# Sums of squares folded on GpSimd, a half tile for the last index columns, and one step moved a slot later in a three-block transformer kernel

## The reference, cut to what matters

```python
def rms_norm(x, g):
    xf = x.astype(jnp.float32)
    y = xf * lax.rsqrt(jnp.mean(xf * xf, axis=-1, keepdims=True) + EPS)
    return (y * g.astype(jnp.float32)).astype(x.dtype)

# block 1: norms, a linear recurrence over chunks (RWKV) and a banded attention
#          beside each other, gates, two branch products, an output product
# block 2:
h = rms_norm(x, norm1_g[l])
proj = jnp.einsum('btd,dc->btc', h, w_in[l])   # q k v | qi (8 heads of 64) ki (64) wi (8) | u v | gates
s = jnp.einsum('bqhd,bsd->bqhs', qi, ki)        # index scores, then top_k picks the keys
score = jnp.einsum('bqh,bqhs->bqs', wi * idx_scale, jax.nn.relu(s))
# ... sparse attention over the picked keys, spatial gating, gates ...
x = x + merged @ w_out[l]
h2 = rms_norm(x, norm2_g[l])
x = x + jnp.square(jax.nn.relu(h2 @ w_ff1[l])) @ w_ff2[l]
x = rms_norm(x, final_g)
# block 3: rmsnorm, input product, pooled mixer and dilated attention, a norm on each,
x = x + jnp.concatenate([y_pool, y_attn], axis=-1) @ w_out[l]
x = x + jnp.square(jax.nn.relu(rmsnorm(x, norm_mlp_g[l]) @ w_up[l])) @ w_down[l]
return rmsnorm(x, norm_final_g)
```

## Time and profile before

| | us |
|---|---|
| median of 3 runs | 3521.14 (3518.85 to 3521.15) |
| the profiled execution | 3520.25 |
| its span, first to last instruction | 3518.5 |
| PE busy in the span | 3405.9 (97%) |
| DVE busy | 2206.8 (63%) |
| ACT busy | 1553.8 (44%) |
| POOL busy | 283.8 (8%) |
| mean granted TensorE clock | 0.986 of full |

### The profile page before, as it was taken

The page is one execution under the profiler, slowest core; times in us unless marked ns, Lnnn a source line. Parts: engine busy times, 40 slices in busy tenths (PEclk is TensorE's granted clock), DMA queues, the critical chain, the costliest instruction groups (busy, mean ns, idle before and its releaser), DMA issues.

```text
span 3518.5 us, 52977 instructions
## 1 busy us (share of the span) xinstructions
PE 3405.9 (97%) x22306; PEld 2958.6 (84%) x22306; DVE 2206.8 (63%) x3056; ACT 1553.8 (44%) x2142; POOL 283.8 (8%) x313
## 2 busy tenths in 40 slices
PE   8999999998989999999999999999999899999998
PEld 7888878777878888788888888888888788888887
DVE  5567655556667576777676446655777766456644
ACT  4445333334543445444544334444444444334444
POOL 3100122220011101101100000001000000000000
PEclk9999999999989999999999999999999999999999
DMA  6554333335634555555555655555554455555654
GB/s 191 183 170 155 129 116 113 109 106 180 193 119 156 186 158 171 168 156 179 185 182 187 195 188 189 191 192 188 164 164 156 156 191 192 191 179 186 198 186 137
DMA packets 587492, 592.47 MB, mean 168 GB/s; under 512 B 20901, under 2 KB 581365, under 8 KB 587126
## 3 DMA queue, kind: packets, MB, share of 16 engines
q1 hardware_dynamic: 587254, 589.08, 52.2%
HBM read 582.72 MB, written 6.32 MB: 167 GB/s over the span
## 4 chain that ended last, share of the span: by engine, by line
PE 89%; DVE 6%; ACT 2%; issue 1%; DMA 1%; SPq 0%; POOL 0%; ACTq 0%; DVEq 0%; POOLq 0%
PE gp L2385 53%; PE gp L2391 28%; PE sidep L1068 4%; DVE w_parts L2314 2%; ACT w_parts L2307 1%; PE sidep L526 0%; DMA high<-bias_rows 0%; DVE stage L2027 0%; ACT lo_half L1940 0%; DVE stage L2031 0%; PE sidep L1308 0%; DMA ring<-w_branch_rwkv 0%; PE sidep L1386 0%; SPq L2141 0%; PE sidep L1645 0%
## 5 line engine op out<-in xcount | busy, mean ns | idle before, releaser
L2314 DVE TENSOR_TENSOR w_parts<-ring,w_parts 128x1024 fp32r<-128x1024 f32 x1084 | 1365.2, 1282 | 427.5 <-ACT w_parts L2307 426.0
L2385 PE MATMUL gp<-x_parts,w_parts 128*128 128x512 f32 x5856 | 1520.8, 400 | 18.5 <-issue 10.6
L2307 ACT ACTIVATE w_parts<-ring 128x1024 fp32r<-128x1024 f32 x1084 | 1108.5, 1053 | 411.6 <-PE gp L2391 405.4
L2385 PEld LDWEIGHTS gp<-x_parts,w_parts 128*128 128x128 f32 x5856 | 1059.8, 191 | 217.3 <-issue 17.7
L2391 PEld LDWEIGHTS gp<-x_parts,w_parts 128*128 128x128 f32 x5856 | 800.1, 192 | 59.3 <-issue 3.0
L2391 PE MATMUL gp<-x_parts,w_parts 128*128 128x256 f32 x5856 | 832.4, 285 | 0.2 <-DVE w_parts L2314 0.2
L2385 PE MATMUL gp<-ff_parts,w_parts 128*128 128x512 f32 x2816 | 707.2, 393 | 4.8 <-ACT w_parts L2307 4.8
L2385 PEld LDWEIGHTS gp<-ff_parts,w_parts 128*128 128x128 f32 x2816 | 506.2, 189 | 96.1 <-ACT w_parts L2307 5.6
L1940 ACT ACTIVATE lo_half<-gp 128x512 f32<-128x512 f32 x255 | 152.3, 597 | 978.8 <-PE gp L2391 978.8
L2027 DVE TENSOR_TENSOR stage<-gp,lo_half 128x512 f32<-128x512 f32 x184 | 127.1, 691 | 466.2 <-ACT lo_half L1940 466.2
L2391 PEld LDWEIGHTS gp<-ff_parts,w_parts 128*128 128x128 f32 x2816 | 383.9, 190 | 27.3
(11 more groups left out here) (374 smaller groups left out, 1671.2 us busy)
## 6 DMA issues: line engine op xcount, KB each, us to landing
ring<-w_in SPq DMA_DIRECT2D x220, 1024.0 KB, 5.1
ring<-w_ff SPq DMA_DIRECT2D x128, 1024.0 KB, 5.8
ring<-w_up SPq DMA_DIRECT2D x64, 1024.0 KB, 5.9
ring<-w_down SPq DMA_DIRECT2D x64, 1024.0 KB, 5.3
ring<-w_out SPq DMA_DIRECT2D x48, 1024.0 KB, 5.3
ring<-w_branch_attn SPq DMA_DIRECT2D x8, 1024.0 KB, 5.1
ring<-w_branch_rwkv SPq DMA_DIRECT2D x8, 1024.0 KB, 6.3
gate_scratch<-stage SPq DMA_DIRECT2D x16, 256.0 KB, 2.3
```

What stands on the lines that cost most here:

```text
L2307: act.activation(w_parts[:, q % PARTS, 0], ring[:, u % RING, SLOT * (q % 2):SLOT * (q % 2) + SLOT, :], ACT.Copy).then_inc(high_split, 1)
L2314: v.tensor_tensor(w_parts[:, q % PARTS, 1], ring[:, u % RING, SLOT * (q % 2):SLOT * (q % 2) + SLOT, :], w_parts[:, q % PARTS, 0].bitcast(F ...
L2385: pe.matmul(gp[:, k % 2, j, :, :], w_parts[:, q % PARTS, 0, c, j * P:(j + 1) * P], operand(s, b, SLOT * n + c), start=(n == 0 and c == 0), ...
```

## The change

Three edits. First, `Rms` gets `folded`: GpSimd also adds the last block's squares, and where a block has two chunks it adds the second chunk's half of the accumulator to the first; TensorE then needs two matmuls of one column and no more. It is on for `norm2`, `mlp3` (both after a section in `next_norm`) and `aout`, and off for `gain_23` (two sets of squares). All these norms' steps on TensorE and VectorE are placed later. Second, the last index block is loaded once as 72 columns (keys, then `wi` on partitions 64 to 71) and multiplied with `j` = 0 only; SyncE copies the scaled keys to the upper partitions with a DMA, `select` starts 1.33 slots later, and its first score also waits for that DMA. Third, in sections of two-slot blocks (`out3a`), the making of the next activations and squares is phase 3 instead of phase 2.

```diff
-            return [(piece(w2_, r * UNIT * P, 3584, 64), 0, 64), (piece(w2_, r * UNIT * P, 3584, 64), 64, 64),
-                    (piece(w2_, r * UNIT * P, 3648, 8), 128, 8)]
+            return [(piece(w2_, r * UNIT * P, 3584, 72), 0, 72)]
...
             def add(self, pool, b):
...
+                if self.folded and b == self.blocks - 1:
+                    pool.wait_ge(self.squared, b + 1)
+                    pool.wait_ge(self.added, b - 1)
+                    for k in range(self.sets):
+                        m = pool.tensor_tensor(self.acc[k], self.acc[k], self.sq[b - 1][k], ALU.add)
+                    m.then_inc(self.added, 1)
+                    if self.chunks == 2:
+                        pool.wait_ge(self.added, b)
+                        for k in range(self.sets):
+                            m = pool.tensor_tensor(self.acc[k][:, 0:TOK], self.acc[k][:, 0:TOK], self.acc[k][:, TOK:2 * TOK], ALU.add)
+                        m.then_inc(self.added, 1)
+
+            def folded_sums(self, pe):
+                pe.wait_ge(self.added, self.blocks - 1 + (self.chunks == 2))
+                for k in range(self.sets):
+                    for t in range(2):
+                        m = pe.matmul(sp_[:, 0, 2 * k + t:2 * k + t + 1], self.acc[k][:, t * P:t * P + P], ones[:, 0:1], ...
...
-        ki, wi = high[:, 7168:7424], high[:, 7424:7680]
+        ki, wi, ki_up = high[0:64, 7168:7424], high[64:72, 7168:7424], high[64:128, 7424:7680]
...
+        def select_sync(sp):
+            yield 0
+            wait_scaled(sp, "index2", 2)
+            sp.dma_start(ki_up, ki).then_inc(ki_copied, 16)
...
             yield 2
             pe.wait_ge(wi_ready, 1)
+            pe.wait_ge(ki_copied, 16)
...
+        def split_phase(s):
+            return 3 if s.slots == 2 else 2
...
+            if s.name in next_norm and phase == split_phase(s):
+                c = slice(2 * b, 2 * b + 2)
+                norm, gain, _ = next_norm[s.name]
+                act.wait_ge(finished, fin_count(s.name, b))
...
-        threads.append(Thread("select", at("qkv2") + 0.34, 0.5, tensor=select_tensor, ...
+        threads.append(Thread("select", at("qkv2") + 1.67, 0.5, sync=select_sync, tensor=select_tensor, ...
...
-            norm = Rms(gain, 8, 2, low, 4096, dst, sets)
+            norm = Rms(gain, 8, 2, low, 4096, dst, sets, folded=(sets == 1))
...
-            return norm.thread(gain, S[name].end, (1.34, 1.67, 2.67, 3.0))
+            return norm.thread(gain, S[name].end, (2.67, 2.67, 4.0, 4.0) if sets == 1 else (2.0, 2.0, 3.34, 3.67))
...
-        aout.thread("aout_rms", first_pair + 3 * PAIR + 8.5, (0, 0.5, 1.5, 2.0))
+        aout.thread("aout_rms", first_pair + 3 * PAIR + 9.5, (0, 0.5, 1.5, 2.0))
...
+                    halves = 1 if s.name == "index2" and b == 2 else 2
                     for c in range(SLOT):
...
-                        for j in range(2):
+                        for j in range(halves):
```

More of the change, by code:

```diff
@@ L474, in build_kernel, with __init__ @@
         class Rms:
-            def __init__(self, name, blocks, chunks, mem, base, dst, sets=1, own=False):
-                self.blocks, self.chunks, self.dst, self.sets = blocks, chunks, dst, sets
+            def __init__(self, name, blocks, chunks, mem, base, dst, sets=1, own=False, folded=False):
+                self.blocks, self.chunks, self.dst, self.sets, self.folded = blocks, chunks, dst, sets, folded
                 self.n = blocks * chunks * P
@@ L514, in add @@
                     m.then_inc(self.added, 1)
+                if self.folded and b == self.blocks - 1:
[13 more added lines that the diff above has]
+                    for t in range(2):
+                        m = pe.matmul(sp_[:, 0, 2 * k + t:2 * k + t + 1], self.acc[k][:, t * P:t * P + P], ones[:, 0:1],
+                                      start=(k == 0 and t == 0), stop=(k == self.sets - 1 and t == 1), skip_group_check=True)
+                m.then_inc(n_summed, 1)
             def tensor_sums(self, pe):
@@ L557, in tensor @@
                     yield places[0]
-                    self.tensor_sums(pe)
+                    if self.folded:
+                        self.folded_sums(pe)
+                    else:
+                        self.tensor_sums(pe)
                     if self.dst:
@@ L1965, in sums_scalar @@
                     m.then_inc(o_gained, 1)
[L1966 to L1972, removed]
                 elif s.name == "down3_1":
@@ L1979, in sums_scalar @@
                     m.then_inc(gained, 1)
+            if s.name in next_norm and phase == split_phase(s):
+                c = slice(2 * b, 2 * b + 2)
+                norm, gain, _ = next_norm[s.name]
+                act.wait_ge(finished, fin_count(s.name, b))
+                for n in (2 * b, 2 * b + 1):
+                    m = act.activation(x_parts[:, n, 0, :], xt[:, n, :], ACT.Copy, scale=gains(gain, n))
+                m.then_inc(x_high_split, 1)
+                norm.square(act, b, xt[:, c, :], lambda i: par("final2", 2 * b + i))
         o_gained = sem("o_gained")
@@ L2255, in build_kernel @@
             att3[th].thread(first_pair + 0.5 * th, 0.6)
-        aout = Rms("aout", 8, 1, low, 8704, [rstd])
+        aout = Rms("aout", 8, 1, low, 8704, [rstd], folded=True)
         threads.append(Thread("ya", first_pair + 7.34, 1.0, scalar=ya_scalar, vector=ya_vector, gpsimd=ya_pool))
-        aout.thread("aout_rms", first_pair + 3 * PAIR + 8.5, (0, 0.5, 1.5, 2.0))
+        aout.thread("aout_rms", first_pair + 3 * PAIR + 9.5, (0, 0.5, 1.5, 2.0))
         norm_after("out3a", "mlp3", [rstd])
```

13 lines of the change are left out of this document (7 added, 6 removed).

## The result

The median of five runs of the changed kernel is 3489.68 us (3489.54 to 3497.02), of the kernel before beside it 3518.85 (3514.76 to 3521.15): ratio 0.9926, interval 0.9915 to 0.9936: 0.7% faster. Forecast was 3495.4, with a range from 3489.5 to 3503; the median lies 0.2 inside its lower end. The profiled execution took 3489.63 (span 3487.9), 30.6 less than that of before.

| stretch | before | after | difference | forecast |
|---|---|---|---|---|
| third block of `index2`, in `index2` | 48.81 | 43.25 | -5.56 | -5.6 |
| first score and `wi`, in `qkv2` | 149.07 | 144.68 | -4.39 | -3.9 |
| `norm2`, in `up2_0` | 181.73 | 180.15 | -1.58 | -1.5 |
| `gain_23`, in `in3` | 211.29 | 211.47 | +0.18 | 0 |
| `aout`, in `out3p` | 52.19 | 51.80 | -0.39 | -0.6 |

The account below looks back on a forecast made before the run. TensorE, 89% of the chain of waits, was taken as the bound. Gains of 5.6 + 4.2 - 0.3 + 14.1 + 2.1 = 25.7 us took the profiled 3520.25 to 3494.6, or 3495.4 as a median; range 3489.5 to 3503.

Parts of the forecast that it names:

- Half tile: Slots 264 to 267, last index block: half of each slot's matmuls go, 5.6 us gained.
- Wait for `wi`: Slot 268: transposes placed later find the scaled block ready, so wait and lower clock go, 4.2 us gained.
- keys: First score in `qkv2`: TensorE waits 0.3 us for the DMA copy of the keys, 3.6 at the upper bound.
- Two-slot blocks and `mlp3`: `out3a` and the sums after it: of 6.0 + 9.6 us lost, 14.1 gained.
- what stays: Loss left in `out3a` and `mlp3`: 0.45 narrow instructions, 0.56 spread, 0.5 for VectorE's lag, 1.5 us in all.
- `norm2`: Norm in `up2_0`: 12 of 16 narrow instructions go, 1.35 us, and 0.15 more for the later spread.
- `gain_23`: Norm in `in3`: keeps its 32 narrow instructions, only placed later, with no wait before: 0 gained.
- `aout`: Norm in `out3p`: four narrow instructions go, 0.45 us; the spread's wait falls from 0.86 to 0.6, 0.15 taken.
- Rival (a): Two-slot blocks stay bound by VectorE, each losing GpSimd's whole 1.45 us add; 5.7 come back: 3501 us, chance 8%.
- Rival (b): The keys come late, costing 5.0 us, or the half tile gives nothing, 5.6: 3501 us, chance 12%.
- Rival (c): Lower clock granted elsewhere behind slot 264: two more stretches give 3499 us, chance 10%; two fewer give 3492.
- Rival (d): Slower: in `out3a` ScalarE and VectorE alternate without overlap, 9.6 us a block, 32 us lost: 3527 us, chance 2%.

Follow-up runs that it names:

- e11: The changed kernel run once more with nothing edited: median 3491.86 us, ratio 0.9922.
- e4: The changed kernel with the full tile of the last index block back and no key copy, late start of `select` kept: median 3499.56 us, ratio 0.9944.
- e6: The changed kernel with the copy of the keys issued one slot later, behind one more load: one run, 3493.97 us.
- e9: The kernel before with only `out3a`'s activations and squares moved to phase 3: median 3506.07 us, ratio 0.9969.
- e2: The changed kernel with folding taken away from all norms, late places kept: median 3493.63 us, ratio 0.993.
- e8: The changed kernel with `gain_23` folded too, its sums and spread at 3.0 and 4.0 slots, and `aout` not folded: median 3494.37 us, ratio 0.9938.
- e3: The changed kernel with folding kept but all sums and spreads at their old, earlier places: median 3502.79 us, ratio 0.9958.
- e5: The changed kernel with `select` started early again at 0.34, half tile and copied keys kept: one run, 3496.47 us.
- e10: The changed kernel, `aout` unfolded, `gain_23` sums and spread at 3.0 and 4.0, GpSimd adding only its last squares: median 3488.64 us, ratio 0.9923.

## Why the prediction was right

The forecast sum was 25.7 us and the stages it spoke of gave 25.6. The time is another matter: 3489.68 is 5.7 under the forecast of 3495.4 and just outside the forecast's own span of 3490 to 3500. Of these 5.7, 2.3 are that the kernel before had a median of 3518.85 beside it and not the 3521.14 that the forecast started from, and 3.5 that the median moved by 29.2 and not by 25.7. What it moved over 25.6 is mostly luck of the granted clock: the profiled execution of the changed kernel has 6.2 us less in `gates` and `v2` that no edit touches. Over the four comparisons the 34 runs of the kernel before average 3517.9, the nine of the changed kernel (with e11) 3491.7. The difference is 26.2. So the sum was right by its mechanism, and that the single median stayed in the range was a near thing.

Step by step:
- *Half tile*, 5.6: measured 5.56, and 5.53 by e4. One half of PSUM written by consecutive matmuls costs them nothing: the slot is exactly half.
- *Wait for `wi`*, 4.2, and *keys*, -0.3, together 3.9: measured 4.39. Slot 268 is 4.55 shorter and 0.16 came back behind it, where I had charged 0.30 for the transposes. VectorE was less late than I had it (block scaled 3.84 us after the slot's start, not 4.2). So the copy was issued at 3.9 instead of 4.3; it landed 3.5 later, at 7.4 (I had 7.2 to 8), and was asked for at 7.9. The 0.3 charged for it did not come. e6 shows that the upper bound of 7.1 was no idle one: 6.4.
- *Two-slot blocks and `mlp3`*, 14.1: measured 13.9. The mechanism was right: e9 gives 12.2 of it by the phase alone, the sums' wait of 3.1 included, which goes since ScalarE is no longer behind, as the prediction had it. It was my expectation of e9 that doubted this, and it fell.
- In what stays, 1.5 forecast and 1.7 measured, two sizes were off against each other: the stall that I put on VectorE's lag (0.5) didn't come, and the fold took 1.60 instead of 0.74 and was waited for 0.53, with 0.21 more at the spread.
- *`norm2`*, 1.5: 1.58. *`gain_23`*, 0: +0.18. *`aout`*, 0.6: 0.39. The four narrow instructions that go are worth the 0.45 forecast (eight cost 0.90 over a bare slot in slot 805, four 0.46 in slot 806 now). The 0.15 for the wait did not come: the spread's wait rose from 0.86 to 0.91 where I had 0.6, since the add on GpSimd lengthens the residual on VectorE (1.24 for 0.69), which the inverse root stands behind. e2 and e8, at the late place without the fold, are 0.48 and 0.46 shorter, with no such wait. That is the one place where folding is a loss.

Rival (a), VectorE bound in the two-slot blocks: its mechanism is real and its place was not. The add falls beside ScalarE's copy and the sum out of PSUM, as argued, and `out3a` shows no wait; that sum, with one input in PSUM, takes its 0.69 beside the add, which takes 1.54 with the end of VectorE's low part of x beside its start. But where a split or the residual on VectorE, with two inputs in SBUF, met one of these adds, the one that began second was lengthened: 1.24 for 0.69 for the residual, 1.60 for 0.74 for the fold, 5.4 for 3.7 for three splits. The Trainium skill ("SBUF — State Buffer", section SBUF: two separate sides) says that whichever starts first holds the shared pair for its whole instruction, and these rows agree, the ends in turn of e8 most plainly. Rival (b) was one position of a DMA away, as e6 shows. Rival (c) came in part, to the good side. Rival (d) did not show. Of the signs listed, one failed: slot 830 took 3.69 and not 3.3, the 0.4 being the wait for the fold.

## What to carry to other kernels

When an in-order engine stands idle for a result while work that others wait for is queued behind it, move the waiting instruction behind that work before looking for faster instructions: one phase's place gave 12.2 of the 25.6 us here, and a wait in the next section went with it. Work handed to an idle engine must be given its place with the duration it has *beside* the others, not alone; folding late gained 1.5 us (e2), at the old places it cost 9.1: e3 is 12.7 above the changed kernel in the three stages (some 6.8 of it at the lower clock behind the waits), e9 without folding 3.6. Compare two traces stage by stage: 6.2 of the 30.6 us between these two came from stretches in which nothing had been changed.

## What the runs showed that I had not expected

- The lower clock comes and goes from one execution to the next in the same code with the same waits: `gates` 350.6 or 353.5, `v2` 111.7 to 116.4, `in3` 209.9 or 211.5 (after and e11 are one program). A wait of 2.56 in the kernel before was followed by such a stretch, one of 2.81 in e5 at the same step was not, and those of 3.1 and 3.92 (e3) and 4.11 (e6) were.
- A wide add on GpSimd and a split on VectorE, side by side, cost both: 3.54 us for two adds of 1.30, and 4.85 for three splits of 1.22 in e10, where the adds took part of the time only.
- A copy of 64 KB within SBUF landed 3.5 us after its issue behind a load well under way and 6.4 behind a load issued 0.4 us earlier; both times 0.2 us after that load itself.
